# Down projections of three feed-forward blocks by seven block products instead of eight, on one Trainium2 core

## The reference, cut to what matters

```
# block 0: d_ff = 2816
gate, up = jnp.split(rms_norm(x, norm_ffn) @ w_gate_up, 2, axis=-1)
x = x + (jax.nn.silu(gate) * up) @ w_down
# blocks 1 and 2: d_ff = 4096
u = jnp.square(jax.nn.relu(rmsnorm(x, mlp_norm) @ w_ff1))
x = x + u @ w_ff2
# at the end
return rmsnorm(x, final_norm)
```

## Time and profile before

| | before |
|---|---|
| median of 3 runs | 1937.71 us (1937.53 to 1937.77) |
| span of the profiled execution, first to last instruction | 1936.4 us |
| TensorE busy | 98% |
| VectorE / ScalarE / GpSimd busy | 51% / 42% / 16% |
| mean granted clock of TensorE | 0.998 |
| moved by DMA | 167.8 MB, 87 GB/s |

### The profile page before, as it was taken

One profiled execution on the slowest core, in us unless ns is written; L12 is line 12 of the kernel. 1 busy time (PEld: TensorE's weight loads), 2 busy tenths in 40 slices (PEclk: granted clock), 3 DMA queues, 4 the chain that ended last, 5 costly groups with the idle time before them and its releaser, 6 DMA issues.

```text
span 1936.4 us, 24529 instructions
## 1 busy us (share of the span) xinstructions
PE 1906.5 (98%) x9718; PEld 1594.4 (82%) x9718; DVE 980.9 (51%) x1549; ACT 810.6 (42%) x1424; POOL 306.1 (16%) x378
## 2 busy tenths in 40 slices
PE   9999999999999999999999999999999999999998
PEld 7888778888888888878898888888878788888887
DVE  5566777522233357589842233337668962223334
ACT  4445876422223235277533232223547743323222
POOL 2133344000000010003412220001002312221000
PEclk9999999999999999999999999999999999999999
DMA  7212111233333322221133333332121224333331
GB/s 240 57 56 93 55 44 45 90 103 93 96 97 98 98 79 65 87 88 45 54 120 98 98 96 93 96 96 89 55 88 44 70 73 125 94 98 96 98 98 55
DMA packets 97138, 167.78 MB, mean 87 GB/s; under 512 B 8160, under 2 KB 49152, under 8 KB 97024
## 3 DMA queue, kind: packets, MB, share of 16 engines
q1 hardware_dynamic: 97024, 166.21, 27.6%
HBM read 164.09 MB, written 2.10 MB: 86 GB/s over the span
## 4 chain that ended last, share of the span: by engine, by line
PE 86%; DVE 5%; ACT 4%; POOL 2%; issue 2%; DMA 0%; SPq 0%; DVEq 0%; POOLq 0%; ACTq 0%
PE ps L49 83%; PE ps L52 3%; DVE wlo L71 2%; ACT sk1h L65 1%; POOL p L71 1%; ACT whi L65 1%; ACT p L62 1%; ACT L62 1%; DVE p L91 1%; POOL hTl L71 1%; DMA raw<-in_w_in_dram 0%; DVE pS L91 0%; DVE rot L71 0%; DVE hTl L71 0%; DVE x L71 0%
## 5 line engine op out<-in xcount | busy, mean ns | idle before, releaser
L65 ACT ACTIVATE whi<-raw 128x1024 fp32r<-128x1024 f32 (+1 forms) x294 | 310.0, 1054 | 728.2 <-PE ps L49 725.0
L71 DVE TENSOR_TENSOR wlo<-raw,whi 128x1024 fp32r<-128x1024 f32 (+1 forms) x294 | 361.0, 1228 | 395.1 <-ACT whi L65 392.1
L49 PE MATMUL ps<-hTh,whi 128*128 128x512 f32 (+1 forms) x1176 | 442.3, 376 | 0.0
L49 PE MATMUL ps<-hTh,wlo 128*128 128x512 f32 (+1 forms) x1176 | 437.7, 372 | 0.0
L49 PE MATMUL ps<-hTl,whi 128*128 128x512 f32 (+1 forms) x1176 | 437.6, 372 | 0.0
L49 PE MATMUL ps<-whi,uh 128*128 128x512 f32 x688 | 268.0, 390 | 0.0
L49 PE MATMUL ps<-whi,ul 128*128 128x512 f32 x688 | 267.7, 389 | 0.0
L49 PE MATMUL ps<-wlo,uh 128*128 128x512 f32 x688 | 267.6, 389 | 0.0
L49 PEld LDWEIGHTS ps<-hTh,wlo 128*128 128x128 f32 x1176 | 220.8, 188 | 39.8
L49 PEld LDWEIGHTS ps<-hTh,whi 128*128 128x128 f32 x1176 | 221.0, 188 | 37.1 <-DVE wlo L71 0.4
L49 PEld LDWEIGHTS ps<-hTl,whi 128*128 128x128 f32 x1176 | 221.1, 188 | 36.4
(11 more groups left out here) (243 smaller groups left out, 2290.4 us busy)
## 6 DMA issues: line engine op xcount, KB each, us to landing
raw<-in_w_ff_dram SPq DMA_DIRECT2D x128, 512.0 KB, 3.6
raw<-in_w_gate_up_dram SPq DMA_DIRECT2D x88, 256.0 KB, 3.1
raw<-in_w_in_dram SPq DMA_DIRECT2D x40, 512.0 KB, 4.6
raw<-in_w_in_dram SPq DMA_DIRECT2D x68, 256.0 KB, 3.1
raw<-in_w_down_dram SPq DMA_DIRECT2D x22, 512.0 KB, 3.5
raw<-in_w_o_dram SPq DMA_DIRECT2D x16, 512.0 KB, 4.3
x<-in_x_dram SPq DMA_DIRECT2D x8, 512.0 KB, 6.5
raw<-in_w_out_dram SPq DMA_DIRECT2D x8, 512.0 KB, 3.9
```

Source lines behind the costliest of these rows:

```text
L49: return self.eng.matmul(out, l, r, start=start, stop=stop, skip_group_check=True)
L65: return self.eng.activation(out, in_, ACT.Copy)
L71: return self.eng.tensor_tensor(out, a, b, op)
```

## The change

The features are taken in pairs p of two k (11, 16 and 16 pairs). A pair's tokens are, for each half r of the tokens (256), a 2 x 2 matrix of blocks A (rows: two tiles of 128 tokens; columns: the two k), and its weights a 2 x 2 matrix B (rows: the two k; columns: halves of 512). The product is made in the form of Winograd with 7 block products and 15 sums, summed over all pairs in PSUM:

- Token sums S2 = A21 + A22 - A11 (`u_basis`, in place, in `u`), S1 = S2 + A11 and S3 = A22 - S2 (`u_sums`), S4 = A12 - S2 (`u_sums_b`), all on VectorE. Four splits per pair: X = (A11, S2), Y = (S1, S3), Z = (A12, A22), and W = S4, which is made for two pairs at once. Their buffers are the four of before and, once the last up matmul is done, eight in the room of `hT` (`token_slots`).
- Weight sums T1 = B12 - B11, T3 = B22 - B12, T2 = B11 + T3, T4 = T2 - B21: GpSimd makes them (`weight_sums`, four instructions a pair) in the up stages, 19 pairs in the first, 12 in each of the others (`job_times`). SyncE brings the raw pair in (1 MB) and takes the sums out to DRAM scratch (1 MB).
- Sweep A over all pairs holds P1 = A11 B11, P5 = S1 T1, P6 = S2 T2, P7 = S3 T3 in the 8 banks: 24 matmuls and two units a pair. Then ScalarE and VectorE copy them out (`kept`, the first part of `down_add`), and sweep B holds P2 = A12 B21, P3 = S4 B22, P4 = A22 T4 in six banks: 18 matmuls and one and a half units a pair. Residual adds of the kept products stand in sweep B at low priority; the tiles get their last adds when sweep B's products end.
- In the last double of sweep B the half r = 0 (tiles 0 and 1) goes first, then r = 1 (tiles 2 and 3).
- The down stages now get their times from the planner (`plan_down`).

```diff
-    htmp = [r.t("htmp%d" % i, [128, 1024]) for i in range(2)]
+    quad = r.t("htmp", [128, 4, 512])
+    htmp = [quad[:, 2 * i:2 * i + 2, :].rearrange("p c n -> p (c n)") for i in range(2)]
+    sdif = [r.t("sdif%d" % i, [128, 2, 2, 128]) for i in range(2)]
+    quads = [quad, u[:, 28:32, :]]
+    wsum = nc.dram_tensor("wsum_dram", [43 * 256, 1024], F32, kind="Internal").ap()
...
-    def rows(w, nk):
-        for k in range(nk):
-            plan.append((1, 1024, [(0, 1024, w[128 * k:128 * k + 128, :].unsqueeze(1))]))
-        return len(plan) - nk
+    needs = {}
+
+    def sums_at(m, p):
+        return 256 * ((0, 11, 27)[m] + p)
+
+    def sweep_a(m, w, nk):
+        first = len(plan)
+        for p in range(nk // 2):
+            o = sums_at(m, p)
+            two = (1, 1024, [(0, 1024, wsum[o:o + 128, :].unsqueeze(1))])
+            one = (1, 1024, [(0, 512, w[256 * p:256 * p + 128, 0:512].unsqueeze(1)),
+                             (512, 512, wsum[o + 128:o + 256, 512:1024].unsqueeze(1))])
+            for unit in ((two, one) if m else (one, two)):
+                needs[len(plan)] = [(m, p)]
+                plan.append(unit)
+        return first
+
+    def sweep_b(m, w, nk):
+        first = len(plan)
+        for p, n in doubles(nk):
+            for q in range(p, p + n):
+                plan.append((1, 1024, [(0, 1024, w[256 * q + 128:256 * q + 256, :].unsqueeze(1))]))
+            o = sums_at(m, p)
+            needs[len(plan)] = [(m, q) for q in range(p, p + n)]
+            plan.append((n, 512, [(0, 512, wsum[o:o + 256 * n, 0:512].rearrange("(a k p) n -> p a k n", k=2, p=128)[:, :, 1, :])]))
+        return first
...
+    BANK = dict(P1=(4, 5), P5=(6, 7), P6=(2, 3), P7=(0, 1), P2=(4, 2), P3=(5, 3), P4=(6, 7))
+    ONE, TWO = ("P7", "P1"), ("P6", "P5")
+    UPB = ((2, 3, 6, 7), (0, 1, 4, 5))
+
+    def a_order(m):
+        np_ = NK[m] // 2
+        steady = TWO + ONE if m else ONE + TWO
+        order = [(p, M, r) for p in range(np_ - 2) for M in steady for r in range(2)]
+        order += [(np_ - 2, M, r) for M in ("P5", "P7") for r in range(2)]
+        order += [(p, M, r) for M in ("P1", "P6") for r in range(2) for p in (np_ - 2, np_ - 1)]
+        return order + [(np_ - 1, M, r) for M in ("P5", "P7") for r in range(2)]
+
+    def a_unit(m, p, M):
+        return U["dn", m] + 2 * p + ((M in TWO) if m == 0 else (M in ONE))
+
+    def b_order(m):
+        ds = doubles(NK[m])
+        order = []
+        for p, n in ds[:-1]:
+            order += [(q, M, r) for q in range(p, p + n) for M in ("P2", "P3") for r in range(2)]
+            order += [(q, "P4", r) for q in range(p, p + n) for r in range(2)]
+        p, n = ds[-1]
+        for r in range(2):
+            order += [(q, M, r) for q in range(p, p + n) for M in ("P2", "P3")] + [(q, "P4", r) for q in range(p, p + n)]
+        return order
...
+        for item in items:
+            edge = item in (("X", 0), ("Y", 0), ("X", 1), ("Y", 1)) or item[0] in "ZW" and of_double(m, item[1])[0] == doubles(NK[m])[-1][0]
+            s = min(range(4 if edge else 12), key=lambda i: (free[i][0], i))
+            slots[item] = (s, free[s][1] or (("up", m, NG[m] - 1, 3, 3) if s >= 4 else None))
+            free[s] = uses[item]
+        return slots
...
+    def job_times(m):
+
+        n = (19, 12, 12)[m]
+        todo = [(f, p) for f in range(3) for p in range(NK[f] // 2)][len(jobs):len(jobs) + n]
+        t0 = T["up", m, 0, 1, 0, 0] if m == 0 else T["up", m, 0, 0, 0, 0]
+        step = (T["upend", m] - (14.0 if m else 8.0) - t0) / n
+        for j, (f, p) in enumerate(todo):
+            q = j % 2 if m == 0 else 1 - j % 2
+            t = t0 + 1.0 + step * j
+            k = (f, p)
+            T["tj", k], T["ts", k], T["tst", k] = t, t + 7.0, t + 13.0
+            jobs.append((m, k, q))
...
+                    sp.wait_ge(*at("tst%d" % q_of[k], k))
                 dst = raw[i % NR][:, 0:nk * n].rearrange("p (k n) -> p k n", k=nk)
                 for j, (o, c, src) in enumerate(pieces):
...
+        def sums_in():
+            for j, (m, k, q) in enumerate(jobs):
+                yield T["tj", k]
+                sp.wait_ge(*at("mm", ("op", m, 3, 1, 1)))
+                if m == 0 and q == 0:
+                    sp.wait_ge(*at("ntr", ("f0", 3, 1)))
+                if job_before(j):
+                    sp.wait_ge(*at("tst%d" % q, job_before(j)))
+                f, p = k
+                w = w_ff2_2[f - 1] if f else w_down[0]
+                for c in range(2):
+                    sp.dma(quads[q][:, 2 * c:2 * c + 2, :].rearrange("p c n -> p (c n)"),
+                           w[256 * p + 128 * c:256 * p + 128 * c + 128, :]).then_inc(*up("tj%d" % q, k if c else None, 16))
+
+        def sums_out():
+            for m, k, q in jobs:
+                yield T["tst", k]
+                o = sums_at(*k)
+                sp.wait_ge(*at("tsum", k))
+                for c in range(2):
+                    sp.dma(wsum[o + 128 * c:o + 128 * c + 128, :],
+                           quads[q][:, 2 * c:2 * c + 2, :].rearrange("p c n -> p (c n)")).then_inc(*up("tst%d" % q, k if c else None, 16))
...
-            for t in range(4):
-                for halves in (((0,), (1,)) if m == 2 and t == 3 else ((0, 1),)):
-                    for k in range(nk - tail, nk):
...
+            for p, M, r in a_order(m):
+                yield T["dn", m, "A", p, M, r]
+                unit, b = a_unit(m, p, M), BANK[M][r]
                 pe.wait_ge(*at("wlo", unit))
+                y = M in ("P5", "P7")
+                pe.wait_ge(*at("ul", (m, "Y" if y else "X", p)))
...
+                for a, c in P3:
+                    ins = pe.mm(ps[b][:, :], st[a][:, c0:c0 + 128], (whi, wlo)[c][unit % NS][:, w0:w0 + 512], p == 0 and (a, c) == (0, 0), p == np_ - 1 and a == 1)
...
+                if q == 0:
+                    pe.wait_ge(*(at("cP", ("P5", m, r)) if M == "P4" else at("xadd", ("U2", m, 0 if M == "P2" else 1))))
...
+        def u_hi(m, kind, keys):
+            slots = token_slots(m)
+            for i, k in enumerate(keys):
+                yield T["uh", (m, kind, k)]
+                s, before = slots[kind, k]
+                act.wait_ge(*(at("uS", (m, k)) if kind in "XZ" else at("sd" if kind == "Y" else "sw", (m, k))))
+                if before:
+                    act.wait_ge(*at("mm", before))
+                n = doubles(NK[m])[i][1] if kind == "W" else 2
+                src = u[:, 2 * k + (kind == "Z"), :] if kind in "XZ" else s_of(i % 2, n)
+                act.copyA(us_(s)[0][:, 0:256 * n], src).then_inc(*up("uh", (m, kind, k)))
...
+        def kept(m):
+            for M in ("P1", "P5", "P7"):
+                for r in range(2):
+                    yield T["cP", (M, m, r)]
+                    act.wait_ge(*at("mm", ("dn", m, "A", NK[m] // 2 - 1, M, r)))
+                    for k, q in last_jobs(m):
+                        act.wait_ge(*at("tst%d" % q, k))
+                    act.copyA(gtmp[r][:, :] if M == "P7" else quad[:, 2 * (M == "P5") + r, :], ps[BANK[M][r]][:, :]).then_inc(*up("cP", (M, m, r)))
...
+                xs = x[:, t, 0:512]
+                dve.tt(xs, xs, quad[:, r, :], ALU.add).then_inc(*up("xadd", ("dn", m, t, 0, "P1")))
...
+                dve.tt(quad[:, r, :], ps[BANK["P6"][r]][:, :], quad[:, r, :], ALU.add).then_inc(*up("xadd", ("U2", m, r)))
...
+        def u_basis(m):
+            for p in range(NK[m] // 2):
+                yield T["uS", m, p]
+                for k in (2 * p, 2 * p + 1):
+                    dve.wait_ge(*at(*u_ready(m, k)))
+                a11, a21 = half_of(u[:, 2 * p, :], 0), half_of(u[:, 2 * p, :], 1)
+                dve.tt(a21, a21, a11, ALU.subtract).then_inc(*up("uS", (m, p, "a")))
+                yield T["uS", m, p] + 0.45
+                dve.wait_ge(*at("uS", (m, p, "a")))
+                dve.tt(a21, a21, half_of(u[:, 2 * p + 1, :], 1), ALU.add).then_inc(*up("uS", (m, p)))
...
+        def u_sums(m):
+            for p in range(NK[m] // 2):
+                yield T["sd", (m, p)]
+                a11, s2 = half_of(u[:, 2 * p, :], 0), half_of(u[:, 2 * p, :], 1)
+                dve.wait_ge(*at("uS", (m, p)))
+                if p >= 2:
+                    dve.wait_ge(*at("ul", (m, "Y", p - 2)))
+                dve.tt(sdif[p % 2][:, 0, :, :], s2, a11, ALU.add)
+                dve.tt(sdif[p % 2][:, 1, :, :], half_of(u[:, 2 * p + 1, :], 1), s2, ALU.subtract).then_inc(*up("sd", (m, p)))
+
+        def u_sums_b(m):
+            ds = doubles(NK[m])
+            for i, (p, n) in enumerate(ds):
+                yield T["sw", (m, p)]
+                dve.wait_ge(*(at("ul", (m, "W", ds[i - 2][0])) if i >= 2 else at("ul", (m, "Y", NK[m] // 2 - 1))))
+                for q in range(p, p + n):
+                    ins = dve.tt(sdif[i % 2][:, q - p, :, :], half_of(u[:, 2 * q + 1, :], 0), half_of(u[:, 2 * q, :], 1), ALU.subtract)
+                ins.then_inc(*up("sw", (m, p)))
...
+        def weight_sums():
```

(64 more changed lines are left out.)

212 lines of the change are left out of this document (146 added, 66 removed).

## The result

The changed kernel takes 1914.34 us (median of four runs, 1913.2 to 1914.91) where the kernel before took 1937.62 (1936.12 to 1937.77) beside it: a ratio of 0.9881 (0.9867 to 0.9895). It is faster by 23.3 us. The prediction said 49.4, and its range ended at 1905.

A forecast was written before the change was run, and what follows sets the result against it. TensorE, busy 98% of the span, was taken as the bound. -58.5 + 1.0 + 5.6 + 1.7 + 0.8 = -49.4 us on 1936.4 gave 1887.0, and with 1.3 for the median 1888.3 us; range 1880 to 1905.

The forecast's parts named there:

- Removed, -58.5.: Down stages: 258 matmuls go at 0.2267 us each, 58.5 us, all on the path.
- VectorE in sweeps A and B, nothing.: VectorE's added work, 4.2 us a pair against TensorE's 5.44 in sweep A, 3.0 against 4.08 in B, is hidden.
- The first rival: VectorE paces sweep A through waits at the splits: 47 us lost, 1935 us, or 1912 if half of it; 14%.
- Sweep A to sweep B, 1.0.: Between the sweeps, a loss of 0.3 us at each of 3 stages, taken as 1.0; bounds 0 to 1.5.
- DMA queue in the down stages, nothing.: Down stages: weight transfers at 193 GB/s, where these stages ran at 97, stay hidden.
- The slower rival: Weight transfers pace the down stages, 12.25 us a pair where it took 10.88: 1996 us; 5%.
- SyncE and GpSimd in the up stages, nothing.: Up stages: a hold of SyncE's queue up to some 16 us and GpSimd's 172 sums cost 0.
- The third rival: The sums hold SyncE or GpSimd in the up stages; 1 us in each of half the pairs is 20 us: 1908; 6%.
- Idle time ahead of the next block, 5.6 for two.: Before `D0` of blocks 1 and 2, TensorE idles 2.8 us each for the late norm, 5.6 in all.
- The rival that the next block absorbs the late norm: The next block waits for other things later on, so only the gain is left: 1880 to 1882; 5%.
- Clock, 1.7.: Half-speed clock behind the idle stretches before blocks 1 and 2, counted once in the two places: 1.7 us, bounds 0 and 3.4.
- End of the kernel, 0.8.: After the last add, scalings of tiles 1 and 2 can stand in the way: 0.8 us, bounds 0 to 2.8.

The follow-up runs named there:

- overlap: The changed kernel with the store of a pair's sums planned behind the next pair's bring-in in blocks 1 and 2: 1896.6 us, ratio 0.9788.
- before_tail1: The kernel before, with only the last 1, not the last 4, of a down stage's k done tile by tile: 1952.68 us, ratio 1.0078.
- overlap_ends: The changed kernel with the store behind the next bring-in, plus reordered instructions around the down-stage ends of blocks 0 and 1: 1890.91 us, ratio 0.9759.
- no_sums: The changed kernel with no weight sums made, brought in or stored, their units filled with raw weights (output not the reference's): 1896.68 us, ratio 0.9789.
- four_norm_buffers: The changed kernel with the final norm's tiles 2 and 3 written to free rows of `u`: 1912.48 us, ratio 0.9867.
- all_three: The changed kernel with the store behind the next bring-in, reordered down-stage ends and the shorter kernel end together: 1889.35 us, ratio 0.9752.
- serial_block0: The changed kernel with the store behind the next bring-in in blocks 1 and 2, but ahead of it in block 0: 1941.17 us, ratio 1.0022.
- overlap_tail: The changed kernel with the store behind the next bring-in, four final norm buffers and the final scalings moved: 1895.73 us, ratio 0.9783.

## Why the prediction was wrong, point by point

- *Removed, -58.5.* Right. 258 instructions went, and both sweeps run without a wait at the spacing of 0.2267 us.
- *VectorE in sweeps A and B, nothing.* Right. It is busy 92% of the window in sweep A, above the 75 to 85% forecast, without a wait of TensorE. The first rival fell.
- *Sweep A to sweep B, 1.0.* No wait there; 0.
- *DMA queue in the down stages, nothing.* Right: 180 to 207 GB/s for 193 forecast, and no wait for weights inside a sweep. (In the up stages it is 234 and 272, for 260.) The slower rival fell.
- *SyncE and GpSimd in the up stages, nothing. This step failed.* "A hold of up to some 16 us costs nothing" was tested against one hold, and none in the up stages is longer than 12.1 us. What counts is that the holds return with every pair, and that the bring-in, the sums and the store form one ring whose turn, 15.3 us, is longer than the planned 14.0. A lead of buffers absorbs one late pair; a ring that is slower than its plan uses any lead up. The step also summed GpSimd's work, 128 of 174 us, as if it were always ready to start, though in the fixed order it waits idle for the transfers; and a sum took 1.30 us alone and 1.43 on average, not 1.04. And the code of the change shows it: with a step over 13 us `T["tst"]` of a pair comes before `T["tj"]` of the next. I compared neither number. The cost, by overlap, was 17.7 us: 8.5 of idle time and most of the rest slow clock. The third rival named the place, at 6% and with 20 us, near what it was, but it too counted only what exceeds 16 us, so its size was right by luck.
- *Idle time ahead of the next block, 5.6 for two.* Mis-sized: 10.1 us after, 11.1 in overlap. The wait ahead of `D0` itself was right, 2.61 and 2.63 us for the 2.8 taken. What the sum lacked are the waits for `wlo` inside `D0`, 4.8 us for both places (1.67, 0.87, 1.03, 1.27), so that even the bound of 4.9 a place was too low. The rival that the next block absorbs the late norm fell. The rows of the kernel after show why, ScalarE first and VectorE second, at the end of the first down stage:

```profile
703.09 0.60 ACT L65 ACTIVATE hTh<-ps 128x512 fp32r<-128x512 f32 x1 [0.34 <-PE ps L52]
705.49 1.06 ACT L62 ACTIVATE htmp<-x 128x1024 f32<-128x1024 f32 x1 [1.80 <-DVE x L71]
...
706.55 0.58 ACT L65 ACTIVATE hTh<-ps 128x512 fp32r<-128x512 f32 x1
```
```profile
703.37 1.41 DVE L79 SCALAR_TENSOR_TENSOR htmp<-x,nsm,gbc 128x512 f32<-128x512 f32 x2
704.70 0.68 DVE L71 TENSOR_TENSOR x<-x,ps 128x512 f32<-128x512 f32 x1
705.29 1.22 DVE L71 TENSOR_TENSOR wlo<-raw,whi 128x1024 fp32r<-128x1024 f32 x1
706.43 0.68 DVE L71 TENSOR_TENSOR x<-x,ps 128x512 f32<-128x512 f32 x1
707.03 1.28 DVE L71 TENSOR_TENSOR hTl<-ps,hTh 128x512 fp32r<-128x512 f32 x2
```

  The second half of tile 0's high part (706.55) stands on ScalarE behind the square of tile 2, which itself waits 1.80 us for VectorE's adds. I added up VectorE's work in those 7 us, but not what stands in ScalarE's order behind a square, nor that the next units' `whi` and `wlo` would be late as well. Before_tail1 gives the norm's own part as 3.7 a place (with tile 0 done 1.36 us later), overlap_ends gets 2.3 of the 5.5 back by order alone.
- *Clock, 1.7.* Mis-sized in the profiled execution, where about 7.7 us were lost, since idle stretches of over 2 us came at four places instead of the two of the sum. In overlap, which keeps the waits at these two, it cost nothing there. What it costs in the median is less sure, as the last section tells.
- *End of the kernel, 0.8.* Mis-sized: 3.4, over the bound of 2.8. I weighed the scalings only. Both norm buffers are still being stored when tiles 2 and 3 want them, which before, with tiles 5.4 us apart, cost nothing. The buffers are worth 1.4 of it and the order of the scalings 0.3. The rest no run separates; in the rows the last add starts 2.24 us after the last matmul (1904.01), where it was 0.43 before, behind an add and a scaling of other tiles.
- *GpSimd beside VectorE.* A `wlo` beside it (1098.73 to 1100.56) slows a sum from 1.30 to 2.17 us, and the reverse holds as well; VectorE and GpSimd of the kernel after:

```profile
1142.01 5.82 DVE L71 TENSOR_TENSOR sdif<-u 128x256 f32<-128x256 f32 x4
```
```profile
1141.76 5.79 POOL L71 TENSOR_TENSOR htmp<-htmp 128x512 f32<-128x512 f32 x4 [4.36 <-DMA htmp<-in_w_ff_dram]
```

  Four token sums take as long as the four weight sums beside them, 1.45 us each, where two alone take 0.76. The rule of the Trainium skill (SBUF — State Buffer, "Who interferes with whom"), that the two exclude each other while an instruction lasts, agrees. But no_sums has no sums and is no faster than overlap, so with the right order this cost nothing, as the prediction took it; with the ring it is part of the 4.32 us wait above.

Without the ring's stalls the time would have been inside the range, 1896.6 us for the 1888.3 forecast, but with the loss twice as large: overlap's span is 1895.7, a loss of 17.8 against the 9.1 of the prediction. 11.1 of it are the two places and 3.4 the end; 3.3 are not assigned.

## What to carry to other kernels

When a load, some work and a store share one in-order queue with other transfers, ask which stands first, this round's store or the next round's load; if the store does, the round is the sum of all three, and its time must be compared with the planned step, not with the lead of one buffer. Where the tiles' ends move closer together, look at every engine's fixed order for an instruction that waits for a later tile ahead of one that the next stage needs, and at each buffer that was free only because the tiles were far apart. In this kernel the work added off the critical path was cheap in busy time; what it cost was the place where it waited.

## What the runs showed of the hardware that was not expected

The clock does not fall after each idle stretch of the same length. In the kernel after it was 0.89 over 705 to 735 us: it fell at about 717 us, behind idle stretches of 2.61 and 1.67 us. In overlap, with 2.60 and 1.67 at the same place and 1.27 behind them, it was 1.00:

```profile
705.00:735.00 30.00, 24.12 (x113) 18.93 (x111) 20.30 (x31) 10.96 (x16) 4.99 (x6) 1.00 0.24 70
```

The wait of 2.2 us in the first mixer, at 272 us, is in every kernel here. In the profiled executions the clock fell behind it in six (before, after, overlap, four_norm_buffers, overlap_ends, all_three) and stayed at 1.00 in four (no_sums, before_tail1, serial_block0, overlap_tail). So what one such stretch costs changes from execution to execution, and a sum can only give it bounds.

In before the time follows the clock. Of 20 timed executions those with a mean clock of 0.999 took 1936.14 to 1936.47 us and those with 0.998 took 1937.57 to 1938.2; the 1.5 us between them are about what the prediction counted for one slow stretch. In the kernel after it does not: the mean clock was 0.992, 0.993, 0.996 and 0.994 at 1914.2, 1914.9, 1914.5 and 1913.2 us. Where the ring of the sums sets the pace, a TensorE that runs at full clock may only reach the next wait sooner; that is argued, since only one of the four has a trace.
